# Layer 1's attention: two condition vectors summed on VectorE, half of the v projection between the heads

## The reference, cut to what matters

```python
mod = silu(c) @ w_ada[layer] + b_ada[layer]          # 6 vectors of 1024: sh1, sc1, g1, sh2, sc2, g2
h = rmsnorm(x, mix_norm_g) * (1 + sc1) + sh1
proj = h @ w_in                                      # q, k, v: 1024 columns each
q = rmsnorm(q, q_g); k = rmsnorm(k, k_g)             # per group of 64 columns
p = softmax(q1 k1 + bias) - lam * softmax(q2 k2 + bias)   # 8 heads, causal in chunks
o = rmsnorm(p @ v, sub_g) * (1 - lam_init)
x = x + g1 * (o @ w_out)
h = rmsnorm(x, ffn_norm_g) * (1 + sc2) + sh2
x = x + g2 * hierarchical_moe(h)                     # 32 experts, 3 matrices of 2.1 MB each, all read
```

## Time and profile before

| | us |
|---|---|
| median of 3 runs | 1254.19 |
| lowest, highest | 1253.91, 1254.9 |
| the profiled execution | 1254.67 |
| its span in the trace | 1252.6 |
| TensorE busy (matmul) | 905.6 (72%) |
| VectorE busy | 316.3 (25%) |
| ScalarE busy | 165.0 (13%) |
| read from HBM | 488.2 MB, 391 GB/s over the span |

### The profile page before, as it was taken

One profiled execution on the slowest core, in us unless ns is written; L12 is line 12 of the kernel. 1 busy time (PEld: TensorE's weight loads), 2 busy tenths in 40 slices (PEclk: granted clock), 3 DMA queues, 4 the chain that ended last, 5 costly groups with the idle time before them and its releaser, 6 DMA issues.

```text
span 1252.6 us, 14496 instructions
## 1 busy us (share of the span) xinstructions
PE 905.6 (72%) x6034; PEld 441.9 (35%) x6034; DVE 316.3 (25%) x848; ACT 165.0 (13%) x395; POOL 21.7 (2%) x70
## 2 busy tenths in 40 slices
PE   5999999565574746566699999967474665665747
PEld 3867554121222312121278554532231212121212
DVE  1288454221212111111131154521111111112011
ACT  1012431000000000000043244300000000000000
POOL 1001100000000000000000000000000000000000
PEclk8999999787878878687899999998787878778779
...
GB/s 363 381 405 355 396 342 370 428 427 428 426 428 428 429 427 429 428 427 428 410 408 209 134 281 324 313 429 427 429 426 429 427 428 429 429 429 429 427 423 263
DMA packets 60586, 490.06 MB, mean 391 GB/s; under 512 B 7649, under 2 KB 8050, under 8 KB 38002
## 3 DMA queue, kind: packets, MB, share of 16 engines
...
HBM read 488.20 MB, written 1.05 MB: 391 GB/s over the span
## 4 chain that ended last, share of the span: by engine, by line
DMA 51%; PE 42%; SPq 3%; DVE 3%; issue 1%; ACT 1%; POOL 0%; DVEq 0%
PE psum L1416 41%; DMA weight_ring<-in_moe_w_down 18%; DMA weight_ring<-in_moe_w_gate 17%; DMA weight_ring<-in_moe_w_up 14%; SPq L455 2%; DMA weight_ring<-in_w_ada 2%; SPq L464 1%; PE psum L1480 0%; DVE h_or_mix_T L990 0%; DVE phase_region L1375 0%; PE psum L1950 0%; DVE phase_region L1401 0%; DVE phase_region L981 0%; DVE h_or_mix_T L1102 0%; DVE phase_region L1093 0%
## 5 line engine op out<-in xcount | busy, mean ns | idle before, releaser
L1416 PE MATMUL psum<-weight_ring,h_or_mix_T 128*32 128x512 f32 (+1 forms) x2240 | 383.5, 713 | 236.2 <-DMA weight_ring<-in_moe_w_gate 146.3
L1416 PEld LDWEIGHTS psum<-weight_ring,h_or_mix_T 128*32 128x32 f32 (+1 forms) x2240 | 119.7, 136 | 486.4 <-issue 483.9
L1416 PE MATMUL psum<-weight_ring,ada_partials 128*32 128x512 f32 x1024 | 138.3, 698 | 78.8 <-DMA weight_ring<-in_moe_w_down 73.8
L1416 PE MATMUL psum<-phase_region 128*128 128x128 f32 (+5 forms) x816 | 153.3, 351 | 3.9 <-DVE x_tokens L1219 1.3
L1416 PEld LDWEIGHTS psum<-phase_region 128*128 128x128 f32 (+2 forms) x816 | 97.4, 188 | 73.7 <-issue 53.5
L1416 PE MATMUL psum<-h_or_mix_T,weight_ring 128*128 128x256 f32 (+1 forms) x520 | 114.0, 377 | 1.5 <-DVE h_or_mix_T L990 1.5
L1416 PEld LDWEIGHTS psum<-h_or_mix_T,weight_ring 128*128 128x128 f32 x520 | 97.3, 190 | 15.4 <-DVE h_or_mix_T L990 1.7
L1416 PEld LDWEIGHTS psum<-weight_ring,ada_partials 128*32 128x32 f32 x1024 | 38.9, 126 | 166.1 <-issue 158.3
L1278 DVE TENSOR_TENSOR phase_region<-psum,gate_rows 128x512 f32<-128x512 f32 x32 | 22.1, 691 | 227.5 <-PE psum L1416 227.5
L1265 DVE SCALAR_TENSOR_TENSOR phase_region<-phase_region,psum 128x512 f32<-128x512 f32 x16 | 11.0, 687 | 246.5 <-ACT phase_region L838 246.5
L838 ACT ACTIVATE phase_region<-psum 128x512 f32<-128x512 f32 x16 | 9.6, 597 | 461.0 <-PE psum L1416 461.0
...
## 6 DMA issues: line engine op xcount, KB each, us to landing
...
```

The costliest lines, as they stand in the source:

```text
L1416: return pe.matmul(out_, lhsT, rhs, start=first, stop=last, **kw)
```

## The change

- Vectors 8 and 9 are summed on VectorE: for each of the 8 slices of the matrix it multiplies 1024 columns by the slice's condition value and adds them to the row so far (`weigh`, into `ROWS`, which is the memory of `PART`). Each step waits for the one before. Steps 0 to 7 of vector 8 follow the q/k rows of u = 8 to 11, two after each; those of vector 9 the rows of u = 14 and 15, two after each, and four behind.
- TensorE then only adds the rows over the partitions (`add_rows`): for vector 8 two matmuls with `ONES` as stationary operand, which give the gate in all partitions at once, without copy and join; for vector 9 eight matmuls with 128 columns of `ROWS` (every eighth) as stationary operand and one moving column.
- v's parts are cut into halves of 4 matmuls (`project_values`). Parts 0 and 1 (both tiles of heads 0 to 3's columns) come before head 0, with the first half of part 2; the rest fills heads 0 to 2. ScalarE takes parts 2 and 3 in heads 0 and 2. VectorE's first head output waits for `first_tile_read`, since v still reads `HT`.
- The sum of vector 10 moves to head 3. Out-projection blocks are dealt out anew over heads 3 to 7 (`early`), with blocks 0 to 3 of unit 2 in heads 5 to 7 (in bank 6 in place of 0).
- The out-projection's slab follows vector 8 in spot 2, vector 11's follows v in spot 0. Slab 11 is issued within `load_experts`, behind unit (2, 0). The last frees come in the order `out_half`, `ada_half`, `ada_summed`, `wout_done`.

```diff
-        fills1 = {0: 8, 1: 9, 2: 10}
-
-        ADA_ORDER = (0, 1, 2, 6, 3, 7, 4, 5, 8, 9, 10, 11)
-        ADA_BANK = (4, 5, 4, 5, 5, 3, 5, 4, 4, 5, 4, 5)
-        JOIN_BANK = {2: 4, 5: 4, 8: 4, 11: 5}
-        COPIED = (2, 6, 7, 5, 8, 11)
-        PART_SLOT = {2: 0, 6: 2, 7: 3, 5: 1, 8: 0, 11: 1}
+
+        ADA_ORDER = (0, 1, 2, 6, 3, 7, 4, 5, 10, 11)
+        WEIGHTED = (8, 9)
+        ADA_BANK = (4, 5, 4, 5, 5, 3, 5, 4, 7, 4, 6, 5)
+        JOIN_BANK = {2: 4, 5: 4, 8: 7, 11: 5}
+        COPIED = (2, 6, 7, 5, 11)
+        PART_SLOT = {2: 0, 6: 2, 7: 3, 5: 1, 11: 1}
...
         def ada(n, at):
+            if n in WEIGHTED:
+                return ("ada", n, at, ada_weighted, WEIGHTED.index(n) + 1)
...
         mid_slabs = [("odd_in", 0, 1, proj_done, 26), ("odd_in", 1, 3, proj_done, 34), ("odd_in", 2, 0, proj_done, 38),
-                     ada(8, 2), ada(9, 1), ada(10, 3), ("odd_out", 0, 0, wout_done, 8), ada(11, 2)]
+                     ada(8, 2), ada(9, 1), ("odd_out", 0, 2, wout_done, 8), ada(10, 3), ada(11, 0)]
         TURNS = [(1, 3, 0, 2), (1, 3, 0, 2)]
...
+                    sp.wait_ge(proj_done, 38)
+                    load_fixed(MID0 + len(mid_slabs) - 1, *mid_slabs[-1][:2])
                 sp.wait_ge(*((conv_out, 1), (scores_done, NH))[L])
                 load_first(0, 0)
 
-                sp.wait_ge(out_half, L + 1)
-                load_first(2, 1)
-                for half in ((1, 0), (0, 1))[L]:
-                    if half == 0:
-                        sp.wait_ge(wout_done, 4 * (L + 1))
-                        load_first(3, 0)
-                    else:
-                        sp.wait_ge(ada_half, L + 1)
-                        load_first(3, 1)
-                sp.wait_ge(ada_summed, sums_by((5, 11)[L]))
-                load_first(4, 0)
...
+                else:
+                    sp.wait_ge(out_half, 2)
+                    load_first(3, 1)
+                    sp.wait_ge(ada_half, 2)
+                    load_first(2, 1)
+                    sp.wait_ge(ada_summed, sums_by(11))
+                    load_first(3, 0)
+                    sp.wait_ge(wout_done, 8)
+                    load_first(4, 0)
 
                 sp.wait_ge(first_quarters, 3 * L + 1)
...
+            def take_values(n):
+                act.wait_ge(proj_done, 18 + 16 + n + 1)
+                half, t = divmod(n, 2)
+                a.copy(Vo[:, t, half * HALF:(half + 1) * HALF], PS[:, 6 if n != 1 else 7, :]).then_inc(v_out, 1)
+
+            for u in range(18):
...
-                if h == 0:
-                    copy_partials(fills1[h])
+                if h in (0, 2):
+                    take_values(2 + h // 2)
...
+                if n == 9:
+                    dve.wait_ge(rows_summed, 2)
+                    v.tensor_tensor(SHIFT[:, st, :], PS[:, ADA_BANK[n], 0:KD], BADA[:, n, :], ALU.add).then_inc(ada_ready, 1)
+                    return
...
+            def weigh(n, lo, hi):
+
+                s = slab_index("ada", n)
+                for k in range(lo, hi):
+                    if k == 0:
+                        dve.wait_ge(slab_in[SPOT[s]], landed(s, 0))
+                        if n == 9:
+                            dve.wait_ge(rows_summed, 1)
+                        ins = v.tensor_scalar(ROWS, wide(s)[:, k, :], CCOL[:, 1, k:k + 1], None, ALU.mult)
+                    else:
+                        if k == ADA_FIRST:
+                            dve.wait_ge(rest_in[SPOT[s]], landed(s, 1))
+                        dve.wait_ge(weight_step, weighed[0])
+                        ins = v.scalar_tensor_tensor(out=ROWS, in0=wide(s)[:, k, :], scalar=CCOL[:, 1, k:k + 1], in1=ROWS,
+                                                     op0=ALU.mult, op1=ALU.add)
+                    if k < KD - 1:
+                        weighed[0] += 1
+                        ins.then_inc(weight_step, 1)
+                    else:
+                        ins.then_inc(ada_weighted, 1)
+
             for u in range(16):
                 dve.wait_ge(qk_rstd, u + 1)
                 dst, gain = (QTo, CV2[:, 24:25]) if u < 8 else (KTo, CV2[:, 22:23])
                 v.scalar_tensor_tensor(out=dst[:, u % 8, :], in0=PS[:, u % 4, 0:S], scalar=gain, in1=RSo[u % 2][:, :],
                                        op0=ALU.mult, op1=ALU.mult).then_inc(qk_out, 1)
+                if 8 <= u < 12:
+                    weigh(8, 2 * (u - 8), 2 * (u - 7))
+                if u == 13:
+                    take_modulation(8)
+                if u > 13:
+                    weigh(9, 2 * (u - 14), 2 * (u - 13))
+
+            weigh(9, 4, KD)
 
...
             def head_out(h):
                 dve.wait_ge(o_rstd, h + 1)
+                if h == 0:
+                    dve.wait_ge(first_tile_read, 1)
                 v.scalar_tensor_tensor(out=HT[:, h, :], in0=PS[:, 3, 0:S], scalar=CV2[:, 23:24], in1=RSo[0][:, :],
                                        op0=ALU.mult, op1=ALU.mult).then_inc(o_out, 1)
 
             biased(0)
             biased(1)
+            take_modulation(9)
...
+            def add_rows(n):
+
+                pe.wait_ge(ada_weighted, WEIGHTED.index(n) + 1)
+                if n == 8:
+                    for half in range(2):
+                        ins = mm(PS[:, 6 + half, :], ONES[:, :], ROWS[:, half * HALF:(half + 1) * HALF], True, True)
+                else:
+                    for k in range(KD):
+                        ins = mm(PS[:, ADA_BANK[n], k:k + 1], ROWS.rearrange("p (q k) -> p k q", k=KD)[:, k, :], ONES[:, 0:1],
+                                 True, True, skip_group_check=True)
+                ins.then_inc(rows_summed, 1)
...
-                before = (2, 1)[L]
+                before = (2, 3)[L]
...
+            def project_values(n, tiles):
+
+                s = slab_index("odd_in", 2)
+                half, t = divmod(n, 2)
+                if n == 0:
                     slab_ready(s)
-                if 4 <= u < 16:
+                    rest_ready(s)
+                    pe.wait_ge(ada_ready, 9)
+                if n > 1 and tiles[0] == 0:
+                    pe.wait_ge(v_out, (1, 3)[n - 2])
+                for k in tiles:
+                    ins = mm(PS[:, 6 if n != 1 else 7, :], HT[:, k, t * P:(t + 1) * P], wide(s)[:, k, half * HALF:(half + 1) * HALF],
+                             k == 0, k == KD - 1, skip_group_check=True)
+                    if n == 3 and k == 0:
+                        ins.then_inc(first_tile_read, 1)
+                if tiles[-1] == KD - 1:
+                    ins.then_inc(proj_done, 1)
+
+            FORE, AFT = range(KD // 2), range(KD // 2, KD)
+            for u in range(16):
+                s = slab_index("odd_in", 0 if u < 8 else 1)
+                if u in (0, 8):
+                    slab_ready(s)
+                if u >= 4:
                     pe.wait_ge(qk_out, u - 3)
-                if u >= 18:
-                    pe.wait_ge(v_out, u - 17)
-                first_of = s if u in (8, 16) else None
+                first_of = s if u == 8 else None
+                if u == 14:
+                    add_rows(8)
...
-                elif u < 16:
+                else:
                     ins = project_T(u % 4, wide(s), (u % 8) * P, first_of)
-                else:
-                    ins = project(6 + u % 2, wide(s), ((u - 16) % 2) * HALF, (u - 16) // 2, first_of)
                 ins.then_inc(proj_done, 1)
-                if 1 <= u <= 16:
+                if u:
                     head_sums(u - 1)
-                if u in (17, 18):
-                    scores(u - 17)
+            project_values(0, FORE)
+            head_sums(15)
+            project_values(0, AFT)
+            project_values(1, FORE)
+            scores(0)
+            project_values(1, AFT)
+            scores(1)
+            pe.wait_ge(qk_rstd, 16)
+            add_rows(9)
+            project_values(2, FORE)
 
...
-            early = {3: range(0, 1), 4: range(1, 3), 5: range(3, 4), 6: range(4, 5), 7: range(5, 6)}
+            early = {3: (range(0, 2), range(0, 2)), 4: (range(2, 3), range(2, 3)),
+                     5: (range(3, 4), range(3, 4), range(0, 2)), 6: (range(4, 5), range(4, 5), range(2, 3)),
+                     7: (range(5, 6), range(5, 6), range(3, 4))}
...
-                if h in fills1:
-                    modulation_sums(fills1[h])
+                if h == 0:
+                    project_values(2, AFT)
+                if h == 1:
+                    project_values(3, FORE)
+                if h == 2:
+                    project_values(3, AFT)
+                if h == 3:
+                    pe.wait_ge(v_out, 4)
+                    modulation_sums(10)
                 if h in early:
-                    pe.wait_ge(o_out, early[h].stop)
-                    for u in range(2):
-                        mix_out(1, u, early[h])
+                    for u, blocks in enumerate(early[h]):
+                        if blocks:
```

(8 more changed lines are left out.)

58 lines of the change are left out of this document (36 added, 22 removed).

## The result

| | us |
|---|---|
| after, median of 20 runs | 1255.59 (1253.49 to 1257.05) |
| before, median of 20 runs beside them | 1253.85 (1252.18 to 1255.44) |
| ratio, 95% interval | 1.0013, 1.0007 to 1.0019 |
| predicted | 1251.0, range 1248.6 to 1255.5 |

What follows compares the result with a forecast made beforehand. Bound taken: when the expert-weight DMA stream can run without a hole, plus fixed bytes at 428 GB/s. TensorE's -6.7 us and the hole's +3.4 made -3.3, from a profiled 1254.67 to 1251.0 us (median 0.5 lower); range 1248.6 to 1255.5.

Steps and rivals of the forecast that it cites:

- the stall: TensorE waiting for VectorE's last weighed step before add_rows(8)'s two matmuls, at about 690.4 us: 0.2 us.
- T: Issue of the expert-weight load waiting for `out_half`, 787.82 us before; forecast 6.7 us earlier, at about 781.1.
- `add_rows(9)`: Vector 9's eight single-column matmuls on TensorE, 16 records: taken at 1.1 us, with 2.05 kept for the range.
- v's half: Half of the v projection on TensorE, 3.5 us; moving one into heads 0 to 2 was to cost nothing.
- The hole: Weight stream empty after T until `ada_half`, because of the order of frees: net +3.3 to +3.4 us.
- Taken away and moved: TensorE: sums of vectors 8 and 9 and a join gone, -8.9 us; moved work saves 1.2 us of head waits.
- VectorE: Weighed steps of 1.25 us each keep up with TensorE until the second scores, costing nothing.
- slack: VectorE's margin before TensorE asks for the second scores' maximum: 10.9 us needed of 11.8, 0.9 us spare.
- The rival of a halved rate: VectorE's weighed step takes two cycles per element, 2.3 us; the kernel is slower at 1261.3 us; chance 6%.
- Waits eat TensorE's gain: Weighed steps of 1.55 us and add_rows(9) at 2.05 cost 2.4 us together: 1253.4 us, no difference; chance 21%.
- the case's bounds: Main case, chance 60%: T earlier by 5.7 to 7.7 us, holes of 2.7 to 4.2, giving 1249.4 to 1252.6.
- the dips: Losses of DMA rate between 788 and 820 us in the kernel before, 1.7 us, forecast to go.

Runs made afterwards that it cites:

- e2: Changed kernel with add_rows(9) reading 128 adjacent columns instead of every eighth, vector 9's shift left permuted: 1251.43 us, 0.9978 of before.
- e1: Changed kernel with one of add_rows(9)'s eight matmuls, shift incomplete: whole time 4656 us, read only up to T, which came at 781.50 us.
- e8: Changed kernel with add_rows(9) on adjacent columns and its eight matmuls done twice, shift permuted: 1255.30 us, 1.0011 of before.
- e3: Changed kernel with 64 equal moving columns instead of one in add_rows(9), strided loads kept: 1255.33 us, 1.0006 of before.
- e5: Changed kernel with the last frees in the order out_half, wout_done, ada_half, ada_summed: 1252.76 us, 0.9986 of before.
- e6: Kernel before with only the changed kernel's order of frees (out_half, ada_half, ada_summed, wout_done): 1256.83 us, 1.0023 of before.

## Why the prediction was wrong

The sum can be redone with its own terms and the measured sizes: -6.7, +2.7 for the row matmuls, +3.1 for v, +0.2 for the stall make -0.7 for T (the traces: -0.84); with a hole of 2.5 that is +1.8, and the medians differ by 1.74. The first point below needs one more line of the kernel before, from the view of its tile `ident`:

```profile
L1416 PEld LDWEIGHTS psum<-ident x16: 186/192/192, 629.6 to 631.3; 128*128 128x128 f32 x16
```

- **`add_rows(9)`: the first failed step.** Put at 1.1 us with 2.05 as its end from above, it took 3.83. The records that gave the upper end (629.61 in the earlier trace rows) load 128 adjacent columns, in 192 ns each (the line above). This one loads every eighth column, in 335 ns. The upper bound was no bound, because its row differed from the new work in the layout too, and not in the size alone. With adjacent columns it is 1.81 (e2), within the bounds. The Trainium skill's figure for a load ("TensorE: Matmul & The Clock Gate", section "LDWEIGHTS"), 107 ns for 128 columns, is close to e2's 113 ns per record and far from the 240 of the strided ones; as a price for adjacent columns it would have been better than my 70.
- **v's half: the second failed step, a term put at nothing.** The half directly behind `add_rows(9)` stands in the sum as it was, at 3.5 us, since TensorE works "without rest from the projections on, at full granted clock". It did work without rest there. But the clock was 0.50 behind the row matmuls, and that half took 6.58 us; the three halves in heads 0 to 2 did take their 3.5. The cost of the new instructions lay as much in the ones behind them as in themselves. That this is the records' doing is shown (e1, e2, e8); that their duration and what they move both have a part in it is shown by e8 against e2 and by e3 against the changed kernel; where the line between a stretch that is harmless and one that isn't lies stays open.
- **The hole: right in mechanism, somewhat large.** 3.4 was forecast. The spans give 2.1 (their difference) - 0.47 + 0.84 = 2.5, e5 2.8 and e6 2.9. Counted by bytes, the stream loses 3.0 us more from T to 820 than before (343 GB/s over 32.6 us against 382 over 32.2, at 428 when nothing is missing). Why the spans give less than that, the traces don't show.
- **Taken away and moved: right.** The three sums' place, the heads (6.3 us for heads 1 and 2 against 6.4), `add_rows(8)` at 1.79 against 1.75, its stall 0.4 against 0.2 (it starts 0.84 us after the head sum at 690.23, the blocks elsewhere 0.43), no waits before heads 4, 6 and 7, one before head 5.
- **VectorE: right in what it decides.** Steps 1.35 instead of 1.25 us, slack 0.4 of 0.9 us left, nobody waits for it beyond the 0.25 us at `add_rows(8)` and the 0.65 us before head 5. The rival of a halved rate is refuted: 1024 elements took 1.28 us, not 2.3. The Trainium skill's sentence on two SBUF sources that aren't bf16 ("Vector Engine (DVE) Microarchitecture Reference", section "Points that are easy to get wrong") would have made it the forecast; this trace doesn't agree with it.
- **The rival nearest in time had the wrong mechanism.** "Waits eat TensorE's gain" gave 1253.4 by VectorE; there was no such wait. Its 0.9 us for `add_rows(9)` were the only part of it that pointed at the place. The prediction's last sentence did name `add_rows(9)` among the two places where it would fail most cheaply.
- **Small slips.** With its own terms the case's bounds come out at 1249.2 and 1252.7, not 1249.4 and 1252.6; and the range's lower end counts the dips as gone once more, though the sum has them gone already. Neither bears on the result.
